# Expert blocks of at most 96 static rows, surplus rows in blocks ahead of the last expert, and the end of the kernel rewritten around them

## What is computed

```
logits = hf @ w_router + b_router;  top_val, top_idx = top_k(logits, 4);  gates = softmax(top_val)
for each of 32 experts e, for the tokens routed to it (512 * 4 = 2048 pairs in all):
    gu   = x @ w1[e] + b1[e]                      # 1024 -> 2048
    gate = min(gu[:, :1024], 7);  up = clip(gu[:, 1024:], -7, 7)
    act  = (up + 1) * gate * sigmoid(1.702 * gate)
    y    = (act @ w2[e] + b2[e])                  # 1024 -> 1024, times the pair's gate
out = rmsnorm(x + sum over a token's 4 pairs)
```

## Time and profile before

| | us |
|---|---|
| median of 2 runs | 2987.49 (2985.16 to 2989.82) |
| profiled execution, device time | 2984.68 |
| its span, first to last instruction | 2982.9 |
| first to last weight load issued by SP in the expert stage | 1898.9 to 2898.3 |
| last matmul of e31 ends | 2940.6 |
| last gathered row added | 2976.8 |

### The profile page before, as it was taken

One profiled execution on the slowest core, in us unless ns is written; L12 is line 12 of the kernel. 1 busy time (PEld: TensorE's weight loads), 2 busy tenths in 40 slices (PEclk: granted clock), 3 DMA queues, 4 the chain that ended last, 5 costly groups with the idle time before them and its releaser, 6 DMA issues. The chain is left out here.

```text
span 2982.9 us, 35137 instructions
## 1 busy us (share of the span) xinstructions
PE 2378.6 (80%) x13231; PEld 1129.2 (38%) x13231; DVE 1392.7 (47%) x3071; ACT 869.3 (29%) x2617; POOL 726.3 (24%) x655
## 2 busy tenths in 40 slices
PE   8998896674436695466678898699999999999994
PEld 4444442241002361124345687433333333333331
DVE  3967777767778866644655333521111111111113
ACT  1143334544454546523533341111000101010001
POOL 0213444433434346433643012100000000000002
PEclk9999997786557797688888899799999999999997
DMA  4349999999999999999999467899999999999996
GB/s 179 117 153 384 408 407 408 415 421 418 418 420 386 416 412 388 420 413 401 408 420 412 187 248 200 325 365 407 419 411 405 420 410 410 412 419 408 413 413 234
DMA packets 149931, 1098.24 MB, mean 368 GB/s; under 512 B 18464, under 2 KB 25888, under 8 KB 50336
## 3 DMA queue, kind: packets, MB, share of 16 engines
q0 software_dynamic: 79232, 553.69, 45.7%
q1 hardware_dynamic: 61952, 530.49, 44.5%
q10 hardware_dynamic: 8576, 11.80, 1.1%
HBM read 1067.60 MB, written 30.93 MB: 368 GB/s over the span
## 5 line engine op out<-in xcount | busy, mean ns | idle before, releaser
L2416 PE MATMUL banks<-arena,spare 128*32 128x512 f32 (+1 forms) x2048 | 473.8, 772 | 430.4 <-ACT spare L2278 423.7
L2049 POOL DMA_INDIRECT arena<-in_expert_uv,picked x512 | 583.0, 1139 | 869.2 <-PE banks L2416 615.4
L2184 DVE SCALAR_TENSOR_TENSOR arena<-arena 128x1024 f32<-128x1024 f32 x384 | 472.8, 1235 | 337.8 <-DMA arena<-in_expert_uv,picked 337.6
L2737 PE MATMUL banks<-arena,aT 128*64 128x512 f32 (+1 forms) x4032 | 614.8, 505 | 17.1 <-DMA arena<-in_expert_w 16.5
L2737 PEld LDWEIGHTS banks<-arena,aT 128*64 128x64 f32 (+1 forms) x4032 | 213.0, 126 | 392.8 <-issue 353.0
L2416 PEld LDWEIGHTS banks<-arena,spare 128*32 128x32 f32 (+1 forms) x2048 | 82.2, 130 | 717.1 <-ACT spare L2278 593.6
L3072 DVE TENSOR_SCALAR aT<-banks 128x512 f32<-128x512 f32 (+1 forms) x49 | 30.1, 615 | 617.4 <-PE banks L2755 617.4
L2749 PE MATMUL banks<-arena,aT 128*64 128x512 f32 (+1 forms) x2016 | 305.2, 502 | 0.6 <-DMA arena<-in_expert_w 0.5
L2670 POOL DMA_INDIRECT picked<-moe_rows,extra x32 | 31.1, 972 | 968.0 <-PE banks L2723 907.1
L2263 ACT ACTIVATE spare<-spare 128x2 f32<-128x2 f32 x256 | 51.9, 203 | 631.7 <-DVE arena L2184 630.9
L2184 DVE SCALAR_TENSOR_TENSOR arena<-arena,extra 128x1024 f32<-128x1024 f32 x128 | 156.5, 1223 | 84.4 <-DMA arena<-in_expert_uv,picked 84.1
(11 more groups left out here) (350 smaller groups left out, 2695.1 us busy)
## 6 DMA issues: line engine op xcount, KB each, us to landing
arena<-in_expert_w SPq DMA_DIRECT2D x192, 2048.0 KB, 34.3
arena<-in_mid_w SPq DMA_DIRECT2D x71, 1024.0 KB, 9.1
expert_rows<-aT ACTq DMA_DIRECT2D x70, 128.0 KB, 8.8
arena<-in_w_q SPq DMA_DIRECT2D x4, 2048.0 KB, 11.6
arena<-in_expert_uv,picked POOLq DMA_INDIRECT x512, 12.6
expert_rows<-arena SPq DMA_DIRECT2D x8, 1024.0 KB, 14.5
arena<-in_w_in SPq DMA_DIRECT2D x3, 2048.0 KB, 13.8
arena<-in_w_out SPq DMA_DIRECT2D x2, 2048.0 KB, 7.8
```

What stands on the lines that cost most here:

```text
L2049: eng.indirect_dma_start(places[place_of[n]], None, uv_rows, bass.IndirectOffsetOnAxis(ap=eidx[:, n:n + 1], axis=0))\
L2184: nc.vector.scalar_tensor_tensor(out=u, in0=u, scalar=1.0, in1=token_rows(tt)[:, g, :], op0=ALU.mult, op1=ALU.mult, accum_out=dots[:, k:k ...
L2416: mm = nc.tensor.matmul(bank[lo:lo + width, sum_bank[tt] + half, :], diag[:, (n + g) % NDIAG, 0:width], places[place_of[n + g]][:, D + hal ...
L2737: mm = nc.tensor.matmul(bank[tile, b_, 0:width], xT[:, c % 2 * 4 + k, r0:r0 + nrows], w[:, k * D + lo:k * D + lo + width], start=c % 2 == ...
```

## The change

`capacity` gives positions 0 to 2 now 96 rows instead of 128. The steps e0 to e30 are as before. The surplus blocks now stand between e30 and the last expert (step e31, position 30), and that last expert's code is the same routine as a surplus block's (`block_of_64`). The loop over surplus blocks is one batch of 32 turns instead of 4 batches of 8.

A surplus block and the last expert use the same six slots of the ring (`placed(FINAL, c)`). The last expert's chunks are loaded when the chunks of the last surplus block are used.

The separate end stage is gone. POOL issues the 16 gathers as soon as e30 and the surplus blocks are stored, into twelve buffers in the slots of e30's c3 to c5. Rows of positions 15 and 30 (steps e30 and e31) are left out of these gathers by an index out of bounds and a gate of zero; they are stored in two DRAM tensors of their own and gathered once each per 128 tokens, in four gathers behind e30's store and four behind e31's. DVE makes the extra lists of indices and gates at the second step (`last_picks`), and puts two adds before e31's gate clip and three more before its `activate`.

```diff
-BATCH = 8
+BATCH = 32
 def capacity(p):
-    return 64 + 32 * (p < 16) + 32 * (p < 3) + 32 * (p == NE - 1)
+    return 64 + 32 * (p < 16) + 32 * (p == NE - 1)
...
-                    for cap, positions in ((64, range(16, NE - 1)), (96, list(range(3, 16)) + [NE - 1])):
+                    for cap, positions in ((64, range(16, NE - 1)), (96, list(range(0, 16)) + [NE - 1])):
                         for q in positions:
-                            sp.dma_start(by_position[cap:P, q, :], any_rows[0:P - cap, q % 2, :]).then_inc(rows_filled, 16)
+                            filled_from = 0 if q in ORDER[-2:] else cap
+                            sp.dma_start(by_position[filled_from:P, q, :], any_rows[0:P - filled_from, q % 2, :]).then_inc(rows_filled, 16)
...
+        FINAL = NE - 1
+        LAST_AT, PREV_AT = ORDER[FINAL], ORDER[FINAL - 1]
+        got = [slot(placed(FINAL - 1, c))[:, j * D:(j + 1) * D] for c in (3, 4, 5) for j in range(4)]
+        late = [slot(placed(FINAL, 0))[:, j * D:(j + 1) * D] for j in range(NT)]
+        prev = [slot(placed(FINAL, 2))[:, j * D:(j + 1) * D] for j in range(NT)]
...
@@ sync
                     for c in range(6):
-                        sp.wait_ge(w_used[c], b + NE)
-                        sp.dma_start(slot(placed(NE, c)), ew[bass.ds(e6 + c, 1), :, :].rearrange("o p n -> p (o n)"))\
-                          .then_inc(w_loaded[placed(NE, c)], 16)
+                        sp.wait_ge(w_used[c], b + FINAL)
+                        sp.dma_start(slot(placed(FINAL, c)), ew[bass.ds(e6 + c, 1), :, :].rearrange("o p n -> p (o n)"))\
+                          .then_inc(w_loaded[placed(FINAL, c)], 16)
+                each_extra(sp, body)
+                used_before = sp.value_load(before_last[0:1, 0:1], min_val=1, max_val=FINAL + NOVER)
+                e6 = sp.value_load(expert_at[0:1, LAST_AT:LAST_AT + 1], min_val=0, max_val=NE - 1) * 6
                 for c in range(6):
+                    i = 6 * FINAL + c
+                    sp.wait_ge(w_used[(i - 9) % 6], (i - 9) // 6 + 1)
+                    sp.wait_ge(w_used[c], used_before)
+                    sp.dma_start(slot(placed(FINAL, c)), ew[bass.ds(e6 + c, 1), :, :].rearrange("o p n -> p (o n)"))\
+                      .then_inc(w_loaded[placed(FINAL, c)], 16)
...
@@ gpsimd
+                n = each_extra(eng, body)
+                eng.wait_ge(x_t, n * 2 + 2 * FINAL)
+                rows_of(LAST_AT)
+                eng.wait_ge(dve_done, dv["gl", 1])
+                eng.wait_ge(y_st[1], stored_rest(FINAL - 1))
+                eng.wait_ge(y_st[0], eng.value_load(before_last[0:1, 1:2], min_val=32 * (FINAL - 1), max_val=32 * (FINAL + NOVER)))
+                for i in range(NPAIR):
+                    if i < NGOT and i % 4 == 0:
+                        eng.wait_ge(w_used[3 + i // 4], FINAL)
+                    if i >= NGOT:
+                        eng.wait_ge(dve_done, end_dv["add", (i - NGOT) // EK, (i - NGOT) % EK])
+                    rows_back(got[i % NGOT], y_dram, Y_ROWS, erow[:, i:i + 1], got_in[i % NGOT])
+                eng.wait_ge(y_st[1], stored_rest(FINAL))
+                eng.wait_ge(y_st[0], n * 32 + 32 * FINAL)
+                eng.wait_ge(w_used[2], n + (FINAL + 1))
+                for tt in range(NT):
+                    rows_back(prev[tt], prev_dram, capacity(PREV_AT), lrow[0][:, tt:tt + 1], prev_rows_in[tt])
+                eng.wait_ge(y_st[0], n * 32 + (32 * FINAL + 32))
+                for tt in range(NT):
+                    rows_back(late[tt], last_dram, 64, lrow[1][:, tt:tt + 1], late_rows_in[tt])
...
@@ tensor, and scalar alike
+                def body(b):
+                    block_of_64(b, hot2, b + 1, True)
+                n = each_extra(eng, body)
+                block_of_64(n, hot[:, LAST_AT:LAST_AT + 1].to_broadcast([3 * NE, 64]), None, False)
...
@@ vector
+                for i in range(BEFORE_CLIP):
+                    add(i)
+                clip_gate(0, 64, n + (FINAL + 1))
+                gated(0, 64, n + (FINAL + 1))
+                for i in range(BEFORE_CLIP, BEFORE_ACT):
+                    add(i)
+                activate(0, 2, n + (FINAL + 1), n * 2 + 2 * FINAL, n * 32 + 32 * FINAL)
+                for i in range(BEFORE_ACT, NPAIR):
+                    add(i)
+                for tt in range(NT):
+                    add_late(tt, prev, prev_rows_in, gl[0], end_dv["add", tt, EK - 1])
+                for tt in range(NT):
+                    add_late(tt, late, late_rows_in, gl[1], end_dv["prev", tt])
+                    if tt:
+                        scale(tt - 1)
+                scale(NT - 1)
```

More of the change, by code:

```diff
@@ L2624, in _ @@
             def _(sp):
[L2625 removed]
+                for s, p in enumerate(ORDER[0:FINAL]):
                     if s == 0:
@@ L2822, in _, with block_of_64 @@
                         bias(YB[1], nrows, 2 * FF, one_hot).then_inc(y_done[1], 1)
[L2824 to L2831, removed]
+                wx = [slot(placed(FINAL, c)) for c in range(6)]
+                def block_of_64(before, one_hot, ready, more):
+                    eng.wait_ge(x_e, before * 2 + (2 * FINAL + 2))
@@ L2839, in body @@
-                    eng.wait_ge(act_ok[0], b * 2 + (2 * NE + 1))
+                            if ready is not None:
+                                eng.wait_ge(hot2_ready, ready)
+                            bias(b_[0], 64, col, one_hot).then_inc(done[0], 1)
+                    if more:
+                        eng.wait_ge(rows_in, before * 16 + 16 * (FINAL + 2))
+                        eng.sem_inc(pe_turn, 1)
+                        transpose_rows(64, 0)
+                    eng.wait_ge(act_ok[0], before * 2 + (2 * FINAL + 1))
@@ L2840, in body @@
                     transpose_act(0, 0)
-                    eng.wait_ge(act_ok[0], b * 2 + (2 * NE + 2))
+                    if more:
+                        transpose_rows(64, 1)
+                    eng.wait_ge(act_ok[0], before * 2 + (2 * FINAL + 2))
                     transpose_act(0, 1)
-                    eng.wait_ge(h_e[0], b * 2 + (2 * NE + 2))
-                    eng.wait_ge(y_out[0], b + NE)
-                    for c in range(4, 6):
-                        eng.wait_ge(w_loaded[placed(NE, c)], b * 16 + loads(NE, c))
-                        out_of(0, 64, c, wx[c]).then_inc(w_used[c], 1)
@@ L2848, in body @@
-                    bias(YB[0], 64, 2 * FF, hot2).then_inc(y_done[0], 1)
-                each_extra(eng, body)
+                    eng.wait_ge(h_e[0], before * 2 + (2 * FINAL + 1))
+                    eng.wait_ge(y_out[0], before + FINAL)
+                    eng.wait_ge(w_loaded[placed(FINAL, 4)], before * 16 + loads(FINAL, 4))
+                    out_of(0, 64, 4, wx[4], range(2))
+                    eng.wait_ge(h_e[0], before * 2 + (2 * FINAL + 2))
+                    out_of(0, 64, 4, wx[4], range(2, 4)).then_inc(w_used[4], 1)
@@ L3110, in body @@
                                             blk2f[0:3 * NE, bass.ds(b, 1)], None, ALU.is_equal).then_inc(hot2_ready, 1)
-                    clip_gate(0, 64, b + (NE + 1))
-                    gated(0, 64, b + (NE + 1))
-                    activate(0, 2, b + (NE + 1), b * 2 + 2 * NE, b * 32 + 32 * NE)
-                each_extra(eng, body)
-        got = [region(j * D, D) for j in range(8)]
-        got_in = [sem(f"got_in{j}") for j in range(8)]
-        stored = sem("stored")
-        dv = steps("dve", [x for tt in range(NT) for x in [("add", tt, k) for k in range(EK)]
-                           + ([("rstd", tt - 1), ("scale", tt - 1)] if tt else [])] + [("rstd", NT - 1), ("scale", NT - 1)])
@@ L3124, in build @@
[L3124 to L3139 removed]
+                    clip_gate(0, 64, b + (FINAL + 1))
@@ new lines, in body, with add @@
+                    gated(0, 64, b + (FINAL + 1))
+                    activate(0, 2, b + (FINAL + 1), b * 2 + 2 * FINAL, b * 32 + 32 * FINAL)
+                    copy_rows(64, b * 2 + (2 * FINAL + 3))
+                n = each_extra(eng, body)
+                def add(i):
+                    tt, k = i // EK, i % EK
+                    eng.wait_ge(got_in[i % NGOT], 16 * (i // NGOT + 1))
+                    if k:
+                        eng.wait_ge(dve_done, end_dv["add", tt, k - 1])
+                    nc.vector.scalar_tensor_tensor(out=h[:, tt, :], in0=got[i % NGOT], scalar=gk_rest[:, i:i + 1],
+                                                   in1=h[:, tt, :], op0=ALU.mult, op1=ALU.add).then_inc(dve_done, 1)
```

216 lines of the change are left out of this document (127 added, 89 removed).

## The result

The changed kernel takes 3028.89 us (median of 2 runs, 3028.76 to 3029.01), against 2987.49 us before: 1.0141 times as long, 95% interval 1.012 to 1.0161. It is slower by 41 us, less than the 2% taken as a difference beforehand, and clear of noise. The forecast was 3025 us, range 2998 to 3052. The profiled execution spans 3026.8 us.

The account below looks back on a forecast made before the run. Weight loads set the pace, then a serial end; skipped turns delay the last expert's loads, then gathers and DVE's adds end the span. 3019.4 less 2982.9 is 36.5, plus 1: 37.5 us on 2987.49 gives 3025 us, range 2998 to 3052.

Parts of the forecast that it names:

- A surplus block would run: Position 0 has 100 rows, over the new limit of 96: one surplus block and six more chunks.
- The 32 rows cost nothing to have: Positions 0 to 2: PE's 9.9 us less for each counted at nothing, since PE only waits longer for weights.
- Small additions early: Extra fills and small DVE operations in the routing chain: 1 us for all, bounds 0 and 6.
- The surplus block takes e31's place: Behind e30: the block runs the last expert's instructions and ends where that expert did before, at 2940.6.
- it does not run dry: Weight queue before the surplus block: still holds e30's chunks until about 2900 while the block's chunks are issued.
- The empty turns: 31 skipped turns before the last expert: 0.80 us each on SP, 0.83 on PE, 24.8 and 25.8 us in all.
- Store and gathers: After the surplus block: store lands in about 2.5 us, gathers start near 2945 beside the weights and end at 2997.2.
- DVE's chain: At the end: last gathered row's add ends 2998.5, then e30's and the last expert's adds, span ends 3019.4.
- The empty turns cost little: Rival, chance 0.17: turns take 0.3 us or less, the queue never empties behind 2930; 3010 us.
- The last expert's own chain decides: Rival, chance 0.13: turns of say 1.1 us on PE, DVE's eleven adds stand behind the last expert's activate; 3035 us.
- the reserve of 2 to 4 us: Last expert's PE chain: its gathers done by 3002, just before DVE asks for them at 3003.9.
- No surplus block runs: Rival, chance 0.04: position 0 has at most 96 rows, late gathers land near 2949; 18 us less, 2970 us.

Follow-up runs that it names:

- e30: Not a run: the kernel's expert step at position 15, 96 rows, just ahead of the surplus blocks; it ended at 2916.82 us before, 2925.40 in the changed kernel.
- e2: Changed kernel with 128 rows at position 0 alone, so no row is surplus, the end still reordered: 2983.18 us, 0.9992 times the kernel before.
- e3: Kernel before with 96 rows at positions 0 to 2 and nothing else changed, one surplus block behind the last expert: 3019.32 us, 1.0113.
- e1: Changed kernel with the surplus loop again in 4 batches of 8 turns: 3016.55 us, 1.0098 times the kernel before.
- e4: Changed kernel with a surplus loop of a single turn, so no empty turn: 3017.78 us, 1.0108 times the kernel before.
- e9: Kernel before with 96 instead of 128 rows at positions 1 and 2 only, so no surplus: 2991.07 us, 1.0014.
- e5: e4 with the last expert's gate clip and activate ahead of all of DVE's adds: 3014.67 us, 1.009 times the kernel before.
- e6: e5 with SP holding back the last expert's c2 to c5 until the surplus block's result is stored: 3019.61 us, 1.0105 times the kernel before.
- e8: e2 with one add ahead of the last expert's gate clip and one more ahead of activate: 2984.58 us, 0.9989 times the kernel before.

## Why the prediction was right

**A surplus block would run.** It did. e2 shows that the block and its turns are the whole loss: without them the changed kernel is level with the one before. e3, e1 and e4 divide it: the block alone is 30 to 33 us, the 31 turns the other 11 to 12.

**The 32 rows cost nothing to have.** Shown by e9, with the 19.7 us found again as waiting. The prediction read two of the stretches of 100 us from 2000 to 2900 as all of them: PE was busy 93.0 to 99.6 us in 100, at 408 to 416 GB/s, not 95.6 to 99.6 at 411 to 415. Most of PE's gaps there are further waits for weights (17.0 us in all from 1950 on, as shown beside e9), so this speaks for the prediction's reading.

**Small additions early, 1 us of 0 to 6.** From the first gather to the one of the step behind e30, it took 957.7 us before and 957.9 in e9, and 958.8 to 961.8 in the nine kernels with the smaller capacity or the new end. The changed kernel had 961.6: 3.9 us more, where 1 stood. Equal programs (e4, e5, e6) differ by 2.7 us in it, so how much of these 1 to 4 us belongs to the change is not shown. On the profiled span the forecast was 3020.4 us and 3026.8 was measured: 5.2 us ahead of the stage, about 3 in it, and 1.6 less behind the surplus block.

**The surplus block takes e31's place.** 23.9 us from start to end, as forecast. The words "it does not run dry" were wrong: with c4 and c5 issued late and only six slots, the DMA engines were at 0.77 in 2920 to 2930. It cost nothing, because PE was behind.

**The empty turns.** 0.65 us on SP and 0.75 on PE for 0.80 and 0.83; 23.1 us on PE for 25.8. The branch figures of the Trainium skill (Advanced Engine Details and Errata, Control Flow Timing) gave an estimated 10 us for the loop, which is half of what SP and less than half of what PE took; the trace does not agree. The Trainium skill (Runtime: NRT & Kernel Launch, Instruction fetch mechanics) has a fetch at each taken branch out of the two-page window; at the 2 us that the prediction put on one, turns of 2.8 us would have shown, and they took 0.65 to 0.75. Whether this jump leaves that window no run shows. What the turns were worth in the end is 11 to 12 us (e1, e4), not 23: most of the time that PE stood in them would have gone into waiting for DVE's adds. What they cost at the end is what the late weights took from the gathers (e4).

**Store and gathers.** Here a term failed. The store was given 2.5 us to land and took 9.8:

```profile
2950.47 0.55 ACTq L2965
2951.19 9.78 DMA expert_rows<-aT
```

These are two pieces of the chain that ended last. SP's six loads were issued from 2948.30, two microseconds ahead, and the store's rows shared the engines with them; e6, where no load is issued meanwhile, has 2.3 to 2.4 us. So the gathers began 12.2 us behind the block's end, and not 4.4. That a store lands in 2.5 us was taken from e31's, which had the engines to itself. The trace before showed the other case too, over all stores of L2878:

```profile
DMA to landing us min/median/max: 2.3/9.8/14.3
```

The rates were about right: 5.57 MB of weights and 1.16 MB of gathers in 2964 to 2980, 348 and 73 GB/s, for 368 and 58.

**DVE's chain.** From the end of the surplus block to the end of the span the prediction had 78.8 us (2940.6 to 3019.4), and it was 77.2 (2949.65 to 3026.8). That agreement is better than its parts. It is in part luck. The gathers began 8 us late, but SP's loads 4 us early (1.4 us ahead of the block's end, for 2.4 behind it, mostly because its turns were shorter), and gathers took a larger share beside the weights; all rows were in by about 3002 (DMA share 0.99 in 3000 to 3002, 0.23 in the next two) where 3006 would be the forecast moved to this trace. The sixteenth add ended at 3006.6, for 3007.5, but not for the reason given: the forecast had it wait for the last row, and from 2991.47 on no add waits for a row; DVE had eleven left to do and did them one behind the other. Behind it 20.2 us, for 20.9.

**The rivals.** "The empty turns cost little" is refuted by the 0.65 and 0.75 us of a turn, and by e1 and e4. "The last expert's own chain decides" did not come true in the changed kernel: PE had the up half done at 2985.6, and DVE's fifth add ended 4.3 us later, at the upper end of the reserve of 2 to 4 us. e5 and e8, where that chain was freed of 17 and 8 us and the end stood, say the same of the kernels without turns and without surplus. "No surplus block runs" was priced at 2970 us; e2 made it true and gave 2983. That price was wrong by 13 us, because it let the late gathers, landing near 2949, set the end. In e2 DVE's sixteen adds ended only at 2959.97, and 20.1 us of its and SP's work followed, for 15.5. That five adds held up the last expert is not the cause: e8 took that away and gained nothing.

What stays open: how much of the early 1 to 4 us belongs to the change at all, and whether it comes from the fills, the added DVE operations, or the rate of the loads; and what a store landing in 2.3 us would be worth if no weights were delayed for it.

## What to carry to other kernels

Where loads set the pace, a block for four rows takes of PE and of the queue what a full one takes (23.9 us and 12.58 MB here), and rows saved elsewhere buy nothing: count blocks and their loads, not rows. A run-time loop in front of the critical work costs its empty turns on every engine, 0.65 us on SP and 0.75 on PE here. The bound has to stay what could occur, so the loop should be left early: batches of 8 (e1) gave as much as a single turn (e4). When work is moved ahead of a wait, follow the in-order engine that has to do it: DVE's adds took PE's time in one place and were themselves the end.

## What the runs showed of the hardware that was not expected

A store of 128 KB with 2 KB pieces took 9.8 us beside weight loads and 2.3 us without them (e6), though it is 0.3 us of bytes at 411 GB/s. After 19.7 us without a matmul, with a granted clock of 0.50 in 2960 to 2970 (1.2 GHz of 2.4), PE's first 32 matmuls took 8.96 us for 7.09, and in the second product, after 5.2 us of standing, 9.44; the granted clock was 0.66 in 2990 to 3000, part of it at the lower level. The longer pause did not cost more: in e1 it was 10.02 us after 4.13 us of standing and 8.25 after 12.13. A turn of the same loop costs PE 0.75 us and POOL 0.45.
